# Expert outputs handed back to their tokens: two fp32r products with a 0/1 matrix in place of one float32 product with weights, and the first transposition of h moved behind the next up product

## The chip, the cores and the metric

The kernel runs on one core of a Trainium2 chip. Its time is the time on the device in microseconds (us), the median of several runs; before the change it is 2474.07 us (three runs, 2473.86 to 2476.77).

## The reference

Two models in a row on 256 tokens of width 1024, all in float32: first two layers with a three-branch mixer, of which the first has a dense SwiGLU and the second a mixture of experts, then two layers with attention. The change lies in the mixture of experts of the second layer. Cut to that:

```python
logits = xf @ w_router                         # 256 tokens, 8 experts
top_logit, top_idx = lax.top_k(logits, 2)
top_w = jax.nn.softmax(top_logit, axis=-1)
# for each expert e, on the tokens that chose it:
y = (silu(xs @ w_gate[e]) * (xs @ w_up[e])) @ w_down[e]     # 1024 -> 2816 -> 1024
out[token] += weight * y                        # each token gets its two experts' rows
x = layernorm(alpha * x + out)
```

## The kernel before

The tokens that chose an expert are worked on in items of up to 128 (CAP) rows. A loop on every engine (`Fori(0, n_items)`) turns once for each item. The weights of an item are 33 panels of 1 MB, in the order gate 0, up 0, gate 1, up 1, gate 2, up 2, down 0, gate 3, up 3, down 1 and so on (11 chunks of 256 hidden columns). SyncE loads each panel into one of seven places when TensorE has given back the panel that was there (L689).

**Precision.** A float32 matmul is done as three fp32r matmuls: each operand is split into a high part (a copy written as fp32r) and a low part (the difference). `mm3` (L1068) issues high x high, high x low, low x high. The high part of a panel is written by ScalarE (`widen`, L1758) and the low part by VectorE (`split_panel`, L2457). Only the first panel of an item is widened by VectorE (L2455). So each panel passes ScalarE, VectorE and TensorE in this order, and every engine takes its instructions strictly as they are listed.

**Gather.** `gather` (L1163) multiplies the tokens, x_tm, with one_hot (1 where a token sits in a row of the item) in plain float32; ScalarE and VectorE split the result into xe_hi and xe_lo.

**Chunks.** For chunk s TensorE computes gate and up (`wide`, L1137) into bank s % 2. ScalarE applies silu (L1762), VectorE multiplies (`product`, L2461), TensorE transposes the product (`turn`, L1146), ScalarE writes the high part of h (`hidden_hi`, L1766), VectorE the low part (`hidden_lo`, L2465). `last` (L1153) multiplies with down and sums all chunks in banks 2 and 3. In a step s TensorE's list is: gate s, turn(s - 1), up s, last(s - 2). ScalarE's list is: widen gate s + 1, hidden_hi(s - 1), widen up s + 1, silu(s), widen down s - 1. VectorE's list is: split gate s + 1, hidden_lo(s - 1), split up s + 1, product(s), split down s - 1. Before the chunk loop both also do up 0, and VectorE gate 0.

**Scatter.** The output of an item is copied from banks 2 and 3 into y_sb by ScalarE at the start of the next turn (`y_out`, L1775). There, behind gate 0 and up 0, TensorE multiplies it with `spread` (L1171): for each of the two blocks of 128 tokens and each of the two halves of the columns one plain float32 matmul of 512 columns, into banks 4 to 7. spread is the transposed `weighted`, a one-hot times the routing weight, which VectorE makes at step 2 (L2511), TensorE transposes near the end of the turn (L1207) and ScalarE copies (L1801). VectorE adds the four results to acc (`accumulate`, L2480) behind the split of up 1. The transpositions of h write banks 6 and 7, so before turn(0) TensorE waits until accumulate has read them (acc_read, L1198). In the first turn spread is zero and banks 2 and 3 are filled by two matmuls (L1188). Behind the loop there is one more scatter and sum, then the layer norm.

Of the kernel before, what the change touches and what calls it, by code (L numbers as in the profile page):

```python
# [20 lines left out]
P = 128  # L21
D = 1024
# [329 lines left out]
mix_mm mixed wout_mm ln_x ln_std ln_z ln_x_done  # L352
router_mm router_w router_exp gu_full act_out h_ready y_full y_read up_full relu_out h_ready_2 y_full_2 y_read_2
counts_mm items_ready one_hot routed_mm xe_hi xe_lo spread split_hi split x_split h_made h_hi mem_std mem_inv mem_x mem_turned mem_xT
panel_wide e_first panel_split e_prod e_turned e_hT_hi y_half y_whole y_sb scatter_mm acc_read
rms_ss rms_std rms_x attn_proj attn_read qk_std qk_ready turnq_mm turnq_act
cmp_tb cmp_h_mm cmp_mid cmp_mid_mm cmp_h cmp_o_mm cmp_kv cmp_k_std cmp_k_ready cmp_kT_mm cmp_kT cmp_v cmp_s_mm cmp_s cmp_e cmp_p
score_mm score_max score_exp pT_mm pT pv_mm pv_read proj2_mm x_done nsa_gates
# [3 lines left out]
def program(nc, weights, consts, attn_consts, cols, mids, rows, ln_rows, x, mem, out):  # L362
    ctx = ExitStack()
    with ctx:
        def sb(name, *shape, stack=ctx, dtype=F32):
            return stack.enter_context(nc.sbuf_tensor(name, [P, *shape], dtype))
# [116 lines left out]
        table = sb("table", ITEMS + 2, stack=moe)  # L483
        table_i = moe.enter_context(nc.sbuf_tensor("table_i", [P, ITEMS + 2], I32))
        one_hot = sb("one_hot", TT, CAP, stack=moe)
        weighted = sb("weighted", TT, CAP, stack=moe)
        spread = sb("spread", TT, P, stack=moe)
        xe_hi = sb("xe_hi", KB, CAP, stack=moe, dtype=F32R)
        ring_more, ring_more_lo = twice_named("ring_more", RING, PANEL, stack=moe)
        y_sb = sb("y_sb", D, stack=moe)  # L490
        acc = sb("acc", TT, D, stack=moe)
        moe.close()
        split.close()

# [219 lines left out]
        def _(pe):  # L714
# [412 lines left out]
            def moe_pe():  # L1127


                def weights_of(part, s, item):  # L1130

                    k = moe_order(part, s)
                    pe.wait_ge(S["panel_split"], item * PER_ITEM + (MIXER_SPLITS + k + 1))
                    panels.step()
                    return panel_hi(k), moe_panel(k, item)[1]

                def wide(part, s, item):  # L1137

                    w = weights_of(part, s, item)
                    o = bank[s % 2][:, (0 if part == "gate" else FCH):][:, 0:FCH]  # L1140
                    for kb in range(KB):
                        ins = mm3(o, (xe_hi[:, kb, :], xe_lo[:, kb, :]), [t[:, kb * PC:(kb + 1) * PC] for t in w], start=(kb == 0), stop=(kb == KB - 1))
                    if part == "up":
                        ins.then_inc(S["gu_full"], 1)

                def turn(s, item):  # L1146

                    pe.wait_ge(S["e_prod"], item * FF_CHUNKS + (s + 1))
                    for m in range(2):
                        ins = pe.transpose(bank[6 + s % 2][:, m * CAP:(m + 1) * CAP], h_tm[:, s % 2, m * P:(m + 1) * P], ident)  # L1150
                    ins.then_inc(S["e_turned"], 1)

                def last(s, item):  # L1153
                    w = weights_of("down", s, item)
                    pe.wait_ge(S["h_ready"], item * FF_CHUNKS + (FF_CHUNKS + s + 1))
                    for h in range(2):
                        for m in range(2):
                            ins = mm3(bank[2 + h][:], [t[:, s % 3, m, 0:CAP] for t in (hT_hi, hT_lo)], [t[:, m * D + h * 512:][:, 0:512] for t in w],
                                      start=(s == 0 and m == 0), stop=(s == FF_CHUNKS - 1 and m == 1))
                        if s == FF_CHUNKS - 1:  # L1160
                            ins.then_inc(S["y_whole"] if h else S["y_half"], 1)

                def gather():  # L1163

                    for kb in range(KB):
                        for tt in range(TT):
                            ins = pe.matmul(bank[4 + kb // 4][:, kb % 4 * CAP:][:, 0:CAP], x_tm[:, tt, kb * P:(kb + 1) * P], one_hot[:, tt, :],  # L1167
                                            start=(tt == 0), stop=(tt == TT - 1))
                    return ins

                def scatter(n):  # L1171

                    pe.wait_ge(S["spread"], n + 1)
                    for h in range(2):
                        pe.wait_ge(S["y_sb"], 2 * n + (h + 1))
                        for tt in range(TT):
                            ins = pe.matmul(bank[4 + 2 * h + tt][:], spread[:, tt, :], y_sb[:, h * 512:(h + 1) * 512], start=True, stop=True)  # L1177
                        ins.then_inc(S["scatter_mm"], 1)

                pe.wait_ge(S["items_ready"], 1)  # L1180
                n_items = pe.value_load(table_i[0:1, 0:1], min_val=N_EXPERTS, max_val=ITEMS)
                pe.wait_ge(S["one_hot"], 1)
                pe.wait_ge(S["ln_x_done"], 2 * DEPTH - 1)
                pe.wait_ge(S["attn_read"], MEM_PANELS)
                gather().then_inc(S["routed_mm"], 1)

                pe.wait_ge(S["spread"], 1)
                pe.matmul(bank[2][:], spread[:, 0, :], x_tm[:, 0, 0:512], start=True, stop=True).then_inc(S["y_half"], 1)  # L1188
                pe.matmul(bank[3][:], spread[:, 0, :], x_tm[:, 0, 0:512], start=True, stop=True).then_inc(S["y_whole"], 1)
                with pe.Fori(0, n_items) as item:  # L1190
                    pe.wait_ge(S["xe_lo"], item + 1)
                    wide("gate", 0, item)
                    wide("up", 0, item)
                    scatter(item)
                    for s in range(1, FF_CHUNKS):
                        wide("gate", s, item)
                        if s == 1:
                            pe.wait_ge(S["acc_read"], item + 2)  # L1198
                        turn(s - 1, item)
                        wide("up", s, item)  # L1200
                        if s >= 2:
                            last(s - 2, item)
                    turn(FF_CHUNKS - 1, item)
                    pe.wait_ge(S["one_hot"], item + 2)
                    gather()
                    for tt in range(TT):
                        ins = pe.transpose(bank[1][:, tt * P:(tt + 1) * P], weighted[:, tt, :], ident)  # L1207
                    ins.then_inc(S["routed_mm"], 1)
                    last(FF_CHUNKS - 2, item)
                    last(FF_CHUNKS - 1, item)  # L1210
                pe.wait_ge(S["xe_lo"], n_items + 1)
                scatter(n_items)
                pe.wait_ge(S["acc_read"], n_items + 2)
# [285 lines left out]
        def _(act):  # L1499
# [247 lines left out]
            def moe_act():  # L1747
# [26 lines left out]

                def y_out(n):  # L1775
                    act.wait_ge(S["y_half"], n + 1)
                    act.activation(y_sb[:, 0:512], bank[2][:], ACT.Copy).then_inc(S["y_sb"], 1)
                    act.wait_ge(S["y_whole"], n + 1)
                    act.activation(y_sb[:, 512:], bank[3][:], ACT.Copy).then_inc(S["y_sb"], 1)

                act.activation(spread[:], cst[:, 0:TT * P].rearrange("p (t k) -> p t k", t=TT), ACT.Copy, scale=0.0).then_inc(S["spread"], 1)
                tokens_hi(0)
# [223 lines left out]
        def _(dve):  # L2006
# [431 lines left out]
            def moe_dve():  # L2438
# [29 lines left out]
                def tokens_lo(n):  # L2468
# [3 lines left out]
                                  xe_hi[:, 4 * h:4 * h + 4, :].bitcast(F32), ALU.subtract)  # L2472
                    ins.then_inc(S["xe_lo"], 1)

                def accumulate(n):
                    for h in range(2):
                        dve.wait_ge(S["scatter_mm"], 2 * n + (h + 1))
                        for tt in range(TT):
                            a = acc[:, tt, h * 512:(h + 1) * 512]
                            ins = tt_(a, a, bank[4 + 2 * h + tt][:], ALU.add)  # L2480
                    ins.then_inc(S["acc_read"], 1)
                    dve.wait_ge(S["acc_read"], n + 2)

                for tt in range(TT):
                    ins = ts_(one_hot[:, tt, :], count, item_pos[:, tt, 0:1], None, ALU.is_equal)
                ins.then_inc(S["one_hot"], 1)
# [3 lines left out]
                with dve.Fori(0, n_items) as item:  # L2490
                    split_panel("gate", 0, item)
                    split_panel("up", 0, item)
                    for s in range(FF_CHUNKS):
                        if s + 1 < FF_CHUNKS:
                            split_panel("gate", s + 1, item)
# [10 lines left out]
                        if s == 2:  # L2506

                            dve.wait_ge(S["routed_mm"], item + 1)
                            for tt in range(TT):
                                ts_(one_hot[:, tt, :], count, item_pos[:, tt, bass.ds(item + 1, 1)], None, ALU.is_equal)  # L2510
                                ins = ts_(weighted[:, tt, :], count, item_pos[:, tt, bass.ds(item, 1)], item_w[:, tt, bass.ds(item, 1)],  # L2511
                                          ALU.is_equal, ALU.mult)
                            ins.then_inc(S["one_hot"], 1)
                    hidden_lo(FF_CHUNKS - 1, item)
                    split_panel("down", FF_CHUNKS - 1, item)
                    tokens_lo(item + 1)
                accumulate(n_items)

            def mlp_dve(kind, l, n_chunks, base, per_step, n_split):
# [499 lines left out]
```

## Time and profile before

| | |
|---|---|
| median of three runs | 2474.07 us |
| time of the profiled execution | 2474.79 us |
| its span, first to last instruction | 2473.0 us |
| mean granted TensorE clock | 0.974 of full speed |
| TensorE busy, matmul | 2371.8 us |
| VectorE busy | 1724.9 us |
| ScalarE busy | 958.3 us |

The profile is of one execution. A busy time is the time in which an engine had an instruction at work; matmuls overlap one another, so their durations are longer than their distance. A view in order of time gives start, duration, engine, line and tiles. Brackets behind a row give how long the engine was idle before it and what released it. The span leaves out 1.8 us around the instructions.

### The profile page before, as it was taken

The page shows a single profiled execution, that of the slowest core. Times are in us where ns is not written, and L with a number is a line of the kernel's source. Part 1 is how long each engine was busy: PE and PEld are TensorE (multiplying, and loading weights), DVE is VectorE, ACT ScalarE, POOL GpSimd, SP SyncE. Part 2 cuts the span into 40 slices and gives each one's busy share as a digit, 9 for nine tenths or more (in the row PEclk, how much of TensorE's full clock was granted, in tenths as well). Part 3 has the DMA queues.
Part 4 walks back from the last instruction along what each step waited for, and adds up shares of the span by engine and source line. Part 5 has one row for each costly group of instructions (what it writes and reads, how often), then busy time and mean ns, then how long its engine had stood idle before and what let it go on. Part 6 is the DMA issues. An engine that isn't in the chain of part 4 may idle for free.

```text
span 2473.0 us, 42815 instructions
## 1 busy us (share of the span) xinstructions
PE 2371.8 (96%) x17534; PEld 2102.8 (85%) x17534; DVE 1724.9 (70%) x1887; ACT 958.3 (39%) x1165; POOL 6.4 (0%) x14
## 2 busy tenths in 40 slices
PE   8999989979999989999999999999999999999998
PEld 6899769977998679899998999998876899876997
DVE  4775267776763378879888798887455777565776
ACT  4324010024333246767667676675234100232000
POOL 0000000000000000000000000000000000000000
PEclk9999999988999989999999999999989999999999
DMA  5222335542322559889898898986421455321454
GB/s 201 104 104 103 119 137 187 187 146 94 120 100 90 204 189 345 334 326 338 336 344 335 324 339 334 345 336 244 166 102 52 156 189 187 131 85 68 174 187 151
DMA packets 68603, 495.18 MB, mean 200 GB/s; under 512 B 7584, under 2 KB 7712, under 8 KB 9104
## 3 DMA queue, kind: packets, MB, share of 16 engines
q1 hardware_dynamic: 67072, 485.57, 53.3%
q0 software_dynamic: 1424, 8.05, 0.9%
q8 instruction: 83, 1.36, 0.2%
q14 instruction: 24, 0.20, 0.0%
HBM read 492.54 MB, written 1.05 MB: 200 GB/s over the span
## 4 chain that ended last, share of the span: by engine, by line
PE 68%; DVE 5%; ACT 1%; issue 1%; DVEq 0%; ACTq 0%
PE wide L336 26%; PE wide L1072 15%; PE wide L1071 15%; PE wide L1167 1%; PE wide L1177 1%; PE wide L892 1%; PE wide L1369 1%; PE wide L1355 1%; PE wide L1150 1%; DVE ring_more_lo L2457 1%; PE wide L1318 0%; PE wide L727 0%; PE wide L1352 0%; DVE ring_hi L2455 0%; DVE ring_lo L2536 0%
## 5 line engine op out<-in xcount | busy, mean ns | idle before, releaser
L336 PE MATMUL wide<-ring_hi,xe_hi 128*128 128x256 f32 x1088 | 315.4, 290 | 7.1 <-DVE ring_more_lo L2457 7.1
L1072 PE MATMUL wide<-ring_hi,xe_lo 128*128 128x256 f32 x1088 | 305.5, 281 | 0.0
L336 PE MATMUL wide<-ring_hi,hT_hi 128*128 128x512 f32 x664 | 262.7, 396 | 2.5 <-DVE ring_lo L2536 2.5
L1072 PE MATMUL wide<-ring_hi,hT_lo 128*128 128x512 f32 x664 | 262.2, 395 | 0.0
L336 PE MATMUL wide<-xT_hi,ring_hi 128*128 128x256 f32 x864 | 244.4, 283 | 7.0 <-DVE xT_lo L2040 4.7
L2457 DVE TENSOR_TENSOR ring_more_lo<-ring_more,ring_hi 128x2048 fp32r<-128x2048 f32 x96 | 219.2, 2290 | 41.2 <-ACT ring_hi L1758 40.2
L2457 DVE TENSOR_TENSOR ring_lo<-ring,ring_hi 128x2048 fp32r<-128x2048 f32 x96 | 219.9, 2290 | 35.0 <-ACT ring_hi L1758 33.6
L1072 PE MATMUL wide<-xT_hi,ring_lo 128*128 128x256 f32 x864 | 244.2, 283 | 0.0
L1071 PE MATMUL wide<-xT_lo,ring_hi 128*128 128x256 f32 x864 | 244.0, 282 | 0.0
L336 PE MATMUL wide<-mix_xT_hi,mix_hi 128*128 128x256 f32 x768 | 229.4, 299 | 5.2 <-DVE xT_lo L2040 5.2
L1071 PE MATMUL wide<-xT_lo,mix_hi 128*128 128x256 f32 x768 | 221.3, 288 | 0.0
L1072 PE MATMUL wide<-mix_xT_hi,ring_lo 128*128 128x256 f32 x768 | 220.8, 287 | 0.0
L336 PEld LDWEIGHTS wide<-ring_hi,xe_hi 128*128 128x128 f32 x1088 | 205.5, 189 | 15.0 <-DVE ring_more_lo L2457 11.0
L2536 DVE TENSOR_TENSOR ring_lo<-ring,ring_hi 128x2048 fp32r<-128x2048 f32 x94 | 215.5, 2292 | 3.2
L1071 PE MATMUL wide<-ring_lo,hT_hi 128*128 128x512 f32 x536 | 210.2, 392 | 0.0
L1721 ACT ACTIVATE gate_s<-wide 128x512 f32<-128x512 f32 x43 | 25.8, 600 | 475.5 <-PE wide L1072 475.5
L1072 PEld LDWEIGHTS wide<-ring_hi,xe_lo 128*128 128x128 f32 x1088 | 206.5, 190 | 0.0
L1071 PE MATMUL wide<-ring_more_lo,xe_hi 128*128 128x256 f32 x704 | 198.3, 282 | 0.0
L336 PE MATMUL wide<-ring,xT 128*128 128x256 f32 (+1 forms) x752 | 188.5, 411 | 1.0 <-DVE xT L2022 1.0
L1758 ACT ACTIVATE ring_hi<-ring 128x2048 fp32r<-128x2048 f32 x96 | 183.5, 1912 | 14.8 <-PE wide L336 14.8
L1758 ACT ACTIVATE ring_hi<-ring_more 128x2048 fp32r<-128x2048 f32 x88 | 168.8, 1919 | 49.9 <-PE wide L336 49.0
L2534 DVE CAST ring_hi<-ring 128x2048 fp32r<-128x2048 f32 x94 | 115.3, 1226 | 102.1 <-DMA ring<-in_weights 101.9
(459 smaller groups left out, 5097.0 us busy)
## 6 DMA issues: line engine op xcount, KB each, us to landing
ring<-in_weights SPq DMA_DIRECT2D x316, 1024.0 KB, 4.8
ring_more<-in_weights SPq DMA_DIRECT2D x120, 1024.0 KB, 4.8
xT<-in_weights SPq DMA_DIRECT2D x24, 1024.0 KB, 4.9
ln_row<-in_ln_rows POOLq DMA_DIRECT2D x4, 1024.0 KB, 6.2
x_tm<-in_x SPq DMA_DIRECT2D x1, 1024.0 KB, 5.9
qkT<-in_mem POOLq DMA_DIRECT2D x1, 1024.0 KB, 5.3
out<-x_tm SPq DMA_DIRECT2D x1, 1024.0 KB, 4.0
cst<-in_consts SPq DMA_DIRECT2D x1, 1009.5 KB, 11.9
```

The lines of the kernel that those rows point to most:

```text
L336: ins = self.pe.matmul(out, lhsT, rhs, start=start, stop=stop)
L892: ins = pe.matmul(o, lhs[hs, h, :], chunk_ident[hs] if turned else rhs[hs, h, :], start=True, stop=True)
L1071: pe.matmul(out, lhsT[0], rhs[1], start=False, stop=False)
L1072: return pe.matmul(out, lhsT[1], rhs[0], start=False, stop=stop)
L1150: ins = pe.transpose(bank[6 + s % 2][:, m * CAP:(m + 1) * CAP], h_tm[:, s % 2, m * P:(m + 1) * P], ident)
L1167: ins = pe.matmul(bank[4 + kb // 4][:, kb % 4 * CAP:][:, 0:CAP], x_tm[:, tt, kb * P:(kb + 1) * P], one_hot[:, tt, :], start=(tt == 0), sto ...
L1177: ins = pe.matmul(bank[4 + 2 * h + tt][:], spread[:, tt, :], y_sb[:, h * 512:(h + 1) * 512], start=True, stop=True)
L1721: act.activation(gate_s[:, slot, :, :], b[:].rearrange("p (m t) -> p m t", m=2), func).then_inc(sems["out"], 1)
L1758: act.activation(panel_hi(k), w, ACT.Copy).then_inc(S["panel_wide"], 1)
L2457: tt_(lo, w, panel_hi(k).bitcast(F32), ALU.subtract).then_inc(S["panel_split"], 1)
L2534: copy(ring_hi[:, slot, :], ring[:, slot, :]).then_inc(S["split_hi"], 1)
L2536: tt_(ring_lo[:, slot, :], ring[:, slot, :], ring_hi[:, slot, :].bitcast(F32), ALU.subtract).then_inc(S["split"], 1)
```

## The change

The matrix that spreads an item's rows to the tokens no longer holds the weights. It is an exact 0/1 matrix (in_slot, transposed into spread), of type fp32r. The item's output is split into y_hi (ScalarE, as y_sb before) and y_lo (VectorE, the new `outputs_lo`), and each of the four products becomes two fp32r matmuls, with y_hi and with y_lo. The routing weight is applied by VectorE: accumulate becomes acc = bank * item_by + acc, with item_by, the column of this item's weights, copied at step 2 of the turn and cleared before the first. outputs_lo stands behind the split of up 0 in the loop, and ahead of the last accumulate behind it. TensorE's turn(0), with the wait for accumulate, moves from between gate 1 and up 1 to behind up 1. The two matmuls that fill banks 2 and 3 ahead of the first turn become four of 256 columns.

```diff
-        weighted = sb("weighted", TT, CAP, stack=moe)
-        spread = sb("spread", TT, P, stack=moe)
+        in_slot = sb("in_slot", TT, CAP, stack=moe)
+        spread = sb("spread", TT, P, stack=moe, dtype=F32R)
+        item_by = sb("item_by", TT, 1, stack=moe)
-        y_sb = sb("y_sb", D, stack=moe)
+        y_hi = sb("y_hi", D, stack=moe, dtype=F32R)
+        y_lo = sb("y_lo", D, stack=moe, dtype=F32R)
@@ TensorE, scatter
-                        pe.wait_ge(S["y_sb"], 2 * n + (h + 1))
+                        pe.wait_ge(S["y_lo"], 2 * n + (h + 1))
                         for tt in range(TT):
-                            ins = pe.matmul(bank[4 + 2 * h + tt][:], spread[:, tt, :], y_sb[:, h * 512:(h + 1) * 512], start=True, stop=True)
+                            pe.matmul(bank[4 + 2 * h + tt][:], spread[:, tt, :], y_hi[:, h * 512:(h + 1) * 512], start=True, stop=False)
+                            ins = pe.matmul(bank[4 + 2 * h + tt][:], spread[:, tt, :], y_lo[:, h * 512:(h + 1) * 512], start=False, stop=True)
@@ TensorE, before the loop
-                pe.matmul(bank[2][:], spread[:, 0, :], x_tm[:, 0, 0:512], start=True, stop=True).then_inc(S["y_half"], 1)
-                pe.matmul(bank[3][:], spread[:, 0, :], x_tm[:, 0, 0:512], start=True, stop=True).then_inc(S["y_whole"], 1)
+                nothing = spread[:].rearrange("p t k -> p (t k)")
+                for b, sem in ((2, "y_half"), (3, "y_whole")):
+                    for h in range(2):
+                        ins = pe.matmul(bank[b][:, h * T:(h + 1) * T], spread[:, 0, :], nothing, start=True, stop=True)
+                    ins.then_inc(S[sem], 1)
@@ TensorE, the chunks
                     for s in range(1, FF_CHUNKS):
                         wide("gate", s, item)
+                        if s > 1:
+                            turn(s - 1, item)
+                        wide("up", s, item)
                         if s == 1:
                             pe.wait_ge(S["acc_read"], item + 2)
-                        turn(s - 1, item)
-                        wide("up", s, item)
+                            turn(0, item)
                         if s >= 2:
                             last(s - 2, item)
@@ VectorE
+                def outputs_lo(n):
+                    for h in range(2):
+                        dve.wait_ge(S["y_sb"], 2 * n + (h + 1))
+                        a = slice(h * 512, (h + 1) * 512)
+                        tt_(y_lo[:, a], bank[2 + h][:], y_hi[:, a].bitcast(F32), ALU.subtract).then_inc(S["y_lo"], 1)
@@ accumulate
-                            ins = tt_(a, a, bank[4 + 2 * h + tt][:], ALU.add)
+                            ins = stt(a, bank[4 + 2 * h + tt][:], item_by[:, tt, :], a, ALU.mult, ALU.add)
@@ the loop
+                dve.memset(item_by[:], 0.0)
                 with dve.Fori(0, n_items) as item:
                     split_panel("gate", 0, item)
                     split_panel("up", 0, item)
+                    outputs_lo(item)
@@ step 2
+                            copy(item_by[:], item_w[:, :, bass.ds(item, 1)])
-                                ins = ts_(weighted[:, tt, :], count, item_pos[:, tt, bass.ds(item, 1)], item_w[:, tt, bass.ds(item, 1)],
-                                          ALU.is_equal, ALU.mult)
+                                ins = ts_(in_slot[:, tt, :], count, item_pos[:, tt, bass.ds(item, 1)], None, ALU.is_equal)
@@ behind the loop
+                outputs_lo(n_items)
                 accumulate(n_items)
```

## Rows read from the trace of the kernel before

**Rows 1.** The page, part 1: busy microseconds, share of span, instructions, by engine.
```profile
PE 2371.8 (96%) x17534; PEld 2102.8 (85%) x17534; DVE 1724.9 (70%) x1887; ACT 958.3 (39%) x1165; POOL 6.4 (0%) x14
```

**Rows 2.** ScalarE in order of time: start, duration, instruction; two turns of the loop.
```profile
1000.89 0.58 ACT L1777 ACTIVATE y_sb<-wide 128x512 f32<-128x512 f32 x1
...
1104.03 0.58 ACT L1777 ACTIVATE y_sb<-wide 128x512 f32<-128x512 f32 x1
```

**Rows 3.** Instructions on tile spread: count, duration min/median/max in ns, first and last start.
```profile
L1177 PE MATMUL wide<-y_sb,spread x72: 590/592/595, 904.6 to 1726.6; 128*128 128x512 f32 x72
L1801 ACT ACTIVATE spread<-wide x8: 391/391/391, 997.0 to 1719.2; 128x256 f32<-128x256 f32 x8
```

**Rows 4.** TensorE's waits in one turn; the same turn's window, DMA share last but one.
```profile
PE wide L336 <- DVE ring_more_lo L2457: 0.4, 1, 0.4
...
1002.00:1104.00 102.00, 102.00 (x722) 94.33 (x723) 86.90 (x66) 70.08 (x60) 0.00 (x0) 1.00 0.89 335
```

**Rows 5.** TensorE in order of time, behind the scatter of the second turn.
```profile
1007.70 3.60 PE L1177 MATMUL wide<-y_sb,spread 128*128 128x512 f32 x8
...
1013.95 0.38 PE L1150 MATMUL wide<-cst,gate_s 128*128 128x128 f32 x2
...
1017.01 0.28 PE L336 MATMUL wide<-ring_hi,xe_hi 128*128 128x256 f32 x1
...
1019.86 0.38 PE L1150 MATMUL wide<-cst,gate_s 128*128 128x128 f32 x2
...
1022.90 0.40 PE L336 MATMUL wide<-ring_hi,hT_hi 128*128 128x512 f32 x1
...
1023.60 0.40 PE L336 MATMUL wide<-ring_hi,hT_hi 128*128 128x512 f32 x1
```

**Rows 6.** ScalarE in order of time, same stretch; idle time before an instruction in brackets.
```profile
1014.36 0.39 ACT L1766 ACTIVATE hT_hi<-wide 128x256 fp32r<-128x256 f32 x1 [4.28 <-PE wide L1150]
1014.64 1.91 ACT L1758 ACTIVATE ring_hi<-ring 128x2048 fp32r<-128x2048 f32 x1
1017.21 0.39 ACT L1762 ACTIVATE gate_s<-wide 128x256 f32<-128x256 f32 x1 [0.66 <-PE wide L1072]
```

**Rows 7.** VectorE in order of time, same stretch.
```profile
1008.32 0.42 DVE L2461 TENSOR_TENSOR gate_s<-gate_s,wide 128x256 f32<-128x256 f32 x1 [1.68 <-ACT gate_s L1762]
...
1010.85 2.47 DVE L2480 TENSOR_TENSOR acc<-acc,wide 128x512 f32<-128x512 f32 x4
1013.45 2.29 DVE L2457 TENSOR_TENSOR ring_lo<-ring,ring_hi 128x2048 fp32r<-128x2048 f32 x1
...
1016.59 2.29 DVE L2457 TENSOR_TENSOR ring_lo<-ring,ring_hi 128x2048 fp32r<-128x2048 f32 x1 [0.51 <-ACT ring_hi L1758]
1018.80 0.42 DVE L2461 TENSOR_TENSOR gate_s<-gate_s,wide 128x256 f32<-128x256 f32 x1
1019.44 2.29 DVE L2457 TENSOR_TENSOR xT_lo<-xT,ring_hi 128x2048 fp32r<-128x2048 f32 x1 [0.22 <-ACT ring_hi L1758]
```

**Rows 8.** Two instructions of VectorE by line: count, duration min/median/max in ns.
```profile
L2471 DVE TENSOR_TENSOR xe_lo<-wide,xe_hi x18: 680/686/692, 891.5 to 1719.9; 128x512 fp32r<-128x512 f32 x18
...
L2583 DVE SCALAR_TENSOR_TENSOR x_tm<-wide,rs,x_tm x8: 740/742/751, 2111.4 to 2467.8; 128x512 f32<-128x512 f32 x8
```

**Rows 9.** ScalarE, VectorE and TensorE in order of time behind the loop.
```profile
1723.75 0.60 ACT L1779 ACTIVATE y_sb<-wide 128x512 f32<-128x512 f32 x1 [0.78 <-PE wide L1072]
...
1727.18 1.29 DVE L2480 TENSOR_TENSOR acc<-acc,wide 128x512 f32<-128x512 f32 x2 [0.43 <-PE wide L1177]
...
1728.52 0.33 PE L1493 MATMUL wide<-cst 128*128 128x128 f32 x1 [1.38 <-DVE acc L2480]
```

**Rows 10.** A TensorE wait of another stage; windows behind pauses, granted clock third from last.
```profile
PE wide L336 <- DVE ring_lo L2536: 2.2, 1, 2.2
...
352.40:355.60 3.20, 3.20 (x17) 3.20 (x17) 3.17 (x3) 0.00 (x0) 0.00 (x0) 0.50 0.90 315
...
1728.60:1732.00 3.40, 3.40 (x17) 3.01 (x18) 2.90 (x8) 0.30 (x1) 0.00 (x0) 1.00 0.60 193
```

More of the change, by code:

```diff
@@ L354 @@
 counts_mm items_ready one_hot routed_mm xe_hi xe_lo spread split_hi split x_split h_made h_hi mem_std mem_inv mem_x mem_turned mem_xT
-panel_wide e_first panel_split e_prod e_turned e_hT_hi y_half y_whole y_sb scatter_mm acc_read
+panel_wide e_first panel_split e_prod e_turned e_hT_hi y_half y_whole y_sb y_lo scatter_mm acc_read
 rms_ss rms_std rms_x attn_proj attn_read qk_std qk_ready turnq_mm turnq_act
@@ L1206, in moe_pe @@
                     for tt in range(TT):
-                        ins = pe.transpose(bank[1][:, tt * P:(tt + 1) * P], weighted[:, tt, :], ident)
+                        ins = pe.transpose(bank[1][:, tt * P:(tt + 1) * P], in_slot[:, tt, :], ident)
                     ins.then_inc(S["routed_mm"], 1)
@@ L1776, in y_out @@
                     act.wait_ge(S["y_half"], n + 1)
-                    act.activation(y_sb[:, 0:512], bank[2][:], ACT.Copy).then_inc(S["y_sb"], 1)
+                    act.activation(y_hi[:, 0:512], bank[2][:], ACT.Copy).then_inc(S["y_sb"], 1)
                     act.wait_ge(S["y_whole"], n + 1)
-                    act.activation(y_sb[:, 512:], bank[3][:], ACT.Copy).then_inc(S["y_sb"], 1)
+                    act.activation(y_hi[:, 512:], bank[3][:], ACT.Copy).then_inc(S["y_sb"], 1)
                 act.activation(spread[:], cst[:, 0:TT * P].rearrange("p (t k) -> p t k", t=TT), ACT.Copy, scale=0.0).then_inc(S["spread"], 1)
```

## The prediction

> **What bounds the kernel now.** I read the page's busy shares first: TensorE is busy for 96% of the span, so a shorter TensorE instruction can only pay where TensorE is the last to be ready [rows 1]. The change lies in the expert loop. The loop's period is the distance between two starts of the same ScalarE instruction one item apart, 1104.03 - 1000.89 = 103.14 us [rows 2], and the copy into spread at the end of each turn occurs 8 times [rows 3]: 8 turns and a ninth scatter behind them. In one turn the view of waits shows TensorE waiting 0.4 us, once, and the window of the same turn a DMA share of 0.89 [rows 4]. So TensorE bounds the loop; the others have slack, VectorE with 86.9 us of 102 the least. Last I read the three engines in order of time over the stretch behind the scatter, since what counts is by how much VectorE and ScalarE are ahead at each handover. Times there are written without the leading 1000.
>
> **What is removed.** The scatter is 8 matmul records in 3.60 us, one of them 592 ns long [rows 3, 5]: the pitch is (3.60 - 0.59)/7 = 0.43, eight of them 3.44 us. The new scatter has 8 fp32r matmuls of 512 columns. The down projection is made of just such ones: three from 22.90 to 23.60, 0.70/3 = 0.232 each [rows 5]; eight make 1.86 us. TensorE's own work falls by 1.58 us an item. If that were all, nine times 1.58 = 14.2 us would go.
>
> **What VectorE gets.** outputs_lo is two instructions of 128x512 from PSUM; the nearest row is xe_lo, 686 ns [rows 8], or 1.29 us for a pair that overlaps by 0.08. They stand behind the split of up 0, and VectorE sits idle there later for 1.68 us before product(0) [rows 7]; 1.29 fits, and y_lo is ready near 5.4, ahead of the scatter at 7.70. The scaled sum takes 742 ns in the same form (PSUM, a column of scalars, SBUF) [rows 8]; four end to end are at most 2.97 us against the present 2.47 [rows 7], with the overlap of before 2.7: +0.25 to +0.5. The copy of item_by and the plainer one-hot are some 0.1 us net in a stretch where VectorE has over 1 us in hand. The ring of slots frees two panels 1.58 earlier and one somewhat later, and no row of TensorE waits for a panel's landing: nothing there. The clearing of item_by and the shorter first products stand once ahead of the loop; bounds 0 and 0.2, I take 0.1.
>
> **What the moved turn costs.** Before, turn(0) stands between gate 1 and up 1, at 13.95; now behind up 1. Its time on TensorE is the same, but on it hangs a chain, which I follow in the rows of before: turn(0) at 13.95; ScalarE's hT_hi at 14.36 (+0.41), which is queued ahead of the widening of up 2, at 14.64 (+0.28), 1.91 long to 16.55; VectorE's split of up 2 at 16.59, 2.29 long; product(1) behind it at 18.80, ending at 19.22 [rows 5 to 7]. TensorE's turn(1) needs product(1). From turn(0) to the end of product(1) this is 19.22 - 13.95 = 5.27 us. Before, TensorE had up 1 and gate 2 to do meanwhile and came to turn(1) at 19.86: 0.64 us after the product, so the chain was hidden.
>
> After: the scatter begins at 7.70 as before; up 1 begins at 13.95 - 1.58 = 12.37; gate 2, of the same 24 products, takes 19.86 - 17.01 = 2.85 [rows 5], so turn(0) is at 15.22 (and 17.01 - 13.95 - 2.85 = 0.21 long). hT_hi 15.63, widening 15.91 to 17.82, split 17.86, product(1) 20.07 to 20.49 (silu(1), behind the widening, is through at 18.2: not the last). The handover back to TensorE is 0.05 behind the last sum of the loop, where nothing had to be loaded [rows 9]; here the weights are the product itself, and I take 0.15. So turn(1) starts at 20.64. TensorE alone would be there at 19.86 - 1.58 = 18.28. It stands still for 2.36 us, and the item is not 1.58 shorter but 20.64 - 19.86 = 0.78 us **longer**. Part of the stall is taken a step earlier: the sum begins at 10.85, ends near 13.6 with the dearer form, and the split of gate 2, which starts at 13.45 now [rows 7], ends at about 16.0, against TensorE's 15.43. That is 0.6 of the same 2.36, not more of it.
>
> What is queued behind these waits: on ScalarE behind hT_hi the widening of up 2, silu(1), down 0, gate 3; on VectorE behind the split of up 2 product(1) and the split of down 0. Carried on at the pitch of 2.2 us a panel (16.59, product in between, 19.44), VectorE has down 0 at 22.7 against TensorE's need at 23.7, gate 3 at 24.9 against 26.4, up 3 at 27.4 against 29.4. Nothing else is late, and after the one-hots VectorE is ahead by more than 1.5 us again. The rest of the turn is TensorE's, moved by +0.78. Bounds of this term: 1.58 less if the chain hid again, and 1 us more if the sum or the split of gate 2 came out on the path too. I take +0.78, 8 times: +6.2.
>
> **The last scatter.** It has nothing to overlap with. Before, the second half of y starts being copied at 1723.75, scatter and sum end at 1728.47, where the norm's statistics and TensorE's 1728.52 follow [rows 9]. After: y_lo's second half from 1724.36 to 1725.04, its four products to 1726.0 and 0.15 to drain, then two sums of 0.74 to 1727.6: -0.8 us.
>
> **Sum.** +6.2 - 0.8 + 0.1 = +5.5 us. The profiled execution took 2474.79 us for its span of 2473.0; it would take 2480.3. The median of the runs shown is 0.7 lower, 2474.07, which gives 2479.6.
>
> **Rivals.** *Faster: the stall does not come.* If hT_hi did not hold up product(1), the whole 1.58 would come through: 8 x 1.58 + 0.8 = 13.4 us, 2460.6. It decides from 1.58 us of slack in the chain; the rows show 0.64 before the turn is moved, and the chain starts 15.22 - 13.95 = 1.27 us later while TensorE comes 1.58 earlier. Only an order other than the listing's would allow it. A weaker form, in which a microsecond of the chain overlaps, gives between -2 and +3.
>
> *Slower by more: the clock falls in the stall.* The pause before turn(1) is 20.64 - 18.9 = 1.7 us long, that before gate 2 0.6. In the dense products of another stage a pause of 2.20 us was followed by a stretch at a granted clock of 0.50, that is 1.2 GHz; after the pause of 1.38 us behind the last scatter the clock stayed at 1.00, 2.4 GHz [rows 9, 10]. 1.7 lies between. A stretch of at least 3.2 us at half speed [rows 10] loses 1.6 us or a little more; in half of the items that is +6.4 to +7, hence 2486; in all, 2493. The Trainium skill, TensorE: Matmul & The Clock Gate, section A second HAM failure mode: psum-queue depth-cycling, says that micro-idles between groups of matmuls, when frequent, make the clock swing between its two levels. By that rule the 16 new pauses would speak for this case; the loop's present pause of 0.4 us an item leaves the clock at 1.00 [rows 4], so the trace agrees only that short ones do no harm.
>
> *Another wait takes over: y_lo holds up the scatter.* It is ready 2.3 us ahead; it would have to cost four times its row. I give it, with the backlog spoiling a later panel (+1 us an item, 2487), a twentieth.
>
> **How the numbers follow.** No change and a change can be told apart here from about 0.2%, 4.9 us: 2469.1 to 2479.0. The main case has 0.57 and spans +3.5 to +7, so that it lies astride this bound: 0.36 of it slower, 0.21 the same. The clock has 0.14 and the other wait 0.05, both slower. The weaker overlap has 0.12, mostly the same, the full gain 0.12. Slower 0.55, same 0.32, faster 0.13. The range takes in main case, most of the weak overlap and the clock in half of the items: 2473 to 2487.
>
> **What would show it.** Scatter records near 1.9 us an item; TensorE's waits for gate_s, ahead of the transposes, near 1.7 us, 8 times, and for a ring_lo split 0.4 to 0.6, 8 times; hT_hi of chunk 0 as much later; a loop period of 103.9; granted clock 1.00 in the loop. I am wrong if the period is under 103.1, or if TensorE shows no pause at the second turn; a clock below 1.00 in the loop would be the second rival.

## The result: 0.2% slower, as forecast

In 17 runs each the median went from 2476.38 us to 2481.39 us; the ratio is 1.002, 95% interval [1.0013, 1.0028]: 5.0 us, between 3.2 and 6.9. That is over the 0.2% named in the prediction by a hair, and clear of zero. The profiled execution took 2480.85 us for a span of 2479.0 us.

The profile of the changed kernel, first the page's span and busy shares. TensorE is busy 9.1 us less than in [rows 1], although the span is 6.0 us longer: work went and waiting came.

```profile
span 2479.0 us, 42850 instructions
PE 2362.7 (95%) x17534; PEld 2105.5 (85%) x17534; DVE 1736.7 (70%) x1914; ACT 957.9 (39%) x1165; POOL 6.4 (0%) x14
```

TensorE's waits over the whole expert loop (engine, line, tile, what it waited for: us in total, times, longest). The first and third are new. The first is turn(1), which waits for product(1); the third is gate 2, which waits for its split. The second is the wait at the start of a turn that [rows 4] show: seven of 0.4 and the first, of 5.6 (4.3 before, which costs nothing: from the write of zeros into spread to the first copy of y it is 11.85 us, 11.84 before).

```profile
PE wide L1152 <- DVE gate_s L2469: 11.4, 8, 1.4
PE wide L336 <- DVE ring_more_lo L2465: 8.4, 8, 5.6
PE wide L336 <- DVE ring_lo L2465: 3.3, 8, 0.4
```

ScalarE in order of time (start, duration, instruction). The first and last row are the copies that [rows 2] gave for before; the two between answer to [rows 6].

```profile
1003.46 0.58 ACT L1785 ACTIVATE y_hi<-wide 128x512 fp32r<-128x512 f32 x1
...
1018.29 0.38 ACT L1774 ACTIVATE hT_hi<-wide 128x256 fp32r<-128x256 f32 x1 [5.58 <-PE wide L1152]
1018.57 1.91 ACT L1766 ACTIVATE ring_hi<-ring 128x2048 fp32r<-128x2048 f32 x1
...
1107.67 0.58 ACT L1785 ACTIVATE y_hi<-wide 128x512 fp32r<-128x512 f32 x1
```

The period of this turn, from one copy of y to the next, is 104.21 us, 1.07 more than before. ScalarE is idle for 5.58 us ahead of hT_hi (4.28 before), because the transposition that it waits for comes later, and the widening of up 2 stands behind it.

TensorE over the same stretch, with [rows 5] for before. Eight scatter products from 1010.31 to 1012.18 take 1.87 us instead of 3.44. Then turn(0) and turn(1); the figures in brackets are TensorE's waits ahead of gate 2 and of turn(1).

```profile
1010.31 0.40 PE L1179 MATMUL wide<-y_hi,spread 128*128 128x512 f32 x1
...
1012.18 0.28 PE L336 MATMUL wide<-ring_hi,xe_hi 128*128 128x256 f32 x1
...
1017.87 0.38 PE L1152 MATMUL wide<-cst,gate_s 128*128 128x128 f32 x2
1018.66 0.38 PE L336 MATMUL wide<-ring_hi,xe_hi 128*128 128x256 f32 x1 [0.41 <-DVE ring_lo L2465]
...
1023.19 0.44 PE L1152 MATMUL wide<-cst,gate_s 128*128 128x128 f32 x2 [1.42 <-DVE gate_s L2469]
```

And VectorE, with [rows 7] for before: y_lo, the scaled sum, the splits of gate 2 and of up 2, product(1). The split of up 2 now waits 1.38 us for its widening, where it waited 0.51.

```profile
1006.61 1.28 DVE L2487 TENSOR_TENSOR y_lo<-wide,y_hi 128x512 fp32r<-128x512 f32 x2
...
1013.47 2.72 DVE L2494 SCALAR_TENSOR_TENSOR acc<-wide,item_by,acc 128x512 f32<-128x512 f32 x4
1016.31 2.29 DVE L2465 TENSOR_TENSOR ring_lo<-ring,ring_hi 128x2048 fp32r<-128x2048 f32 x1
...
1020.51 2.29 DVE L2465 TENSOR_TENSOR ring_lo<-ring,ring_hi 128x2048 fp32r<-128x2048 f32 x1 [1.38 <-ACT ring_hi L1766]
1022.72 0.41 DVE L2469 TENSOR_TENSOR gate_s<-gate_s,wide 128x256 f32<-128x256 f32 x1
```

Behind the loop (ScalarE's copy, then VectorE; [rows 9] for before) there was a gain. The copy of the second half of y starts at 1733.56, y_lo's second half runs 1734.19 to 1734.88, and the norm's statistics start at 1737.61: 4.05 us behind the copy instead of 4.75.

```profile
1733.56 0.60 ACT L1787 ACTIVATE y_hi<-wide 128x512 fp32r<-128x512 f32 x1 [0.79 <-PE wide L1074]
...
1734.19 0.69 DVE L2487 TENSOR_TENSOR y_lo<-wide,y_hi 128x512 fp32r<-128x512 f32 x1 [0.70 <-ACT y_hi L1787]
1734.80 2.77 DVE L2494 SCALAR_TENSOR_TENSOR acc<-wide,item_by,acc 128x512 f32<-128x512 f32 x4
1737.61 2.47 DVE L2336 BATCH_NORM_STATS2 stat<-acc 128x6 f32<-128x512 f32 x4
```

For the comparisons below I measure two more things in each trace. The **stage** is the time from ScalarE's write of zeros into spread to the first norm statistics behind the loop; it holds all that the change touches but the clearing of item_by (0.06 us). The **pitch** is the mean distance of two products of 256 columns that follow each other in the second turn, 20 us behind the copy of y and later (some 360 to 380 distances). The **period** and the positions of turn(0) and turn(1) are those of the second turn, counted from the start of the copy of y.

| kernel | median us | ratio to before, 95% | turn(0) | turn(1) | pitch ns | period | stage |
|---|---|---|---|---|---|---|---|
| before | 2476.38 | | 13.06 | 18.97 | 117.8 | 103.14 | 845.7 |
| changed | 2481.39 | 1.002 [1.0013, 1.0028] | 14.41 | 19.73 | 118.6 | 104.21 | 853.2 |
| turn(0) in its old place | 2474.89 | 0.9992 [0.9983, 1.0001] | 12.92 | 18.86 | 118.6 | 103.23 | 845.3 |
| the move alone | 2499.05 | 1.0081 [1.0068, 1.0095] | 15.92 | 21.23 | 117.8 | 105.48 | 867.1 |
| up 2 widened first | 2471.2 | 0.9978 [0.9969, 0.9987] | 14.46 | 18.30 | 118.6 | 102.74 | 841.5 |
| sum in halves | 2467.0 | 0.9959 [0.9946, 0.9973] | 11.58 | 17.50 | 118.6 | 101.93 | 835.5 |
| item_by padded | 2483.09 | 1.0025 [1.0015, 1.0035] | 14.38 | 19.69 | 118.2 | 103.99 | 851.6 |
| before plus 8 bytes | 2482.89 | 1.0021 [1.0012, 1.003] | 13.10 | 19.00 | 118.6 | 103.39 | 847.6 |
| halves and padded | 2471.87 | 0.9966 [0.9952, 0.9981] | 11.54 | 17.48 | 118.2 | 101.79 | 834.1 |
| item_by in stat | 2479.83 | 1.0015 [1.0006, 1.0024] | 14.32 | 19.63 | 117.8 | 103.88 | 850.8 |
| halves, item_by in stat | 2459.88 | 0.9935 [0.9921, 0.9949] | 11.53 | 17.49 | 117.8 | 101.77 | 833.6 |

Each ratio is to the kernel before on the same chip, so it is the number to compare, not the median.

### The profile page after: what moved, and what is told of

It reads as the page before. It is cut to its first block, busy times and chain, and to the rows that moved or that the text cites. A ratio compares the mean times of both kernels' runs of the same rounds, so it can differ in the third digit from the quotient of the medians.

```text
span 2479.0 us, 42850 instructions
## 1 busy us (share of the span) xinstructions
PE 2362.7 (95%) x17534; PEld 2105.5 (85%) x17534; DVE 1736.7 (70%) x1914; ACT 957.9 (39%) x1165; POOL 6.4 (0%) x14
## 4 chain that ended last, share of the span: by engine, by line
PE 67%; DVE 5%; issue 2%; ACT 2%; DVEq 0%; ACTq 0%
PE wide L336 26%; PE wide L1074 15%; PE wide L1073 15%; PE wide L1169 1%; PE wide L894 1%; PE wide L1377 1%; PE wide L1152 1%; PE wide L1363 1%; DVE ring_more_lo L2465 1%; ACT ring_hi L1766 1%; PE wide L1360 1%; PE wide L1326 0%; PE wide L729 0%; DVE ring_hi L2463 0%; PE wide L1337 0%
```

## The experiments

**1. Is it the move? The change without it.**

```diff
                         wide("gate", s, item)
-                        if s > 1:
-                            turn(s - 1, item)
-                        wide("up", s, item)
                         if s == 1:
                             pe.wait_ge(S["acc_read"], item + 2)
-                            turn(0, item)
+                        turn(s - 1, item)
+                        wide("up", s, item)
```

> The change without its move: fp32r scatter, weight in the sum, but turn(0) between gate 1 and up 1 as before. Theory (the moved turn starts a chain over hT_hi, the widening and split of up 2 and product(1), and turn(1) waits for its end): turn(0) now waits for the sum, which ended 12.73 us behind the copy of y in the changed kernel, so it stands at about 12.8 instead of 14.4 (13.06 before); TensorE then reaches turn(1) at about 18.8 without a wait (18.97 before, 19.73 changed). Loop period 103.2 (102.9 if the 0.3 us that the changed kernel loses behind turn(1) goes too), against 104.21; time 2 to 10 us under the changed kernel and within 3 us of the kernel before. Rival (the fp32r scatter or outputs_lo, not the move, cost the item its 1.07 us): the period stays near 104.2.

turn(0) came at 12.92 and turn(1) at 18.86, with no wait between them. The waits of TensorE show one new line only, turn(0) waiting for the sum:

```profile
PE wide L1152 <- DVE acc L2492: 9.1, 8, 1.1
PE wide L336 <- DVE ring_more_lo L2463: 8.4, 8, 5.5
```

The stage is 8.0 us shorter than the changed kernel's. So the loss is the move's. But without the move the gain of 1.58 us is not there either: turn(0) comes only 0.14 us earlier than before, so the wait for the sum takes 1.4 of it (the view shows 1.1, since it counts from the end of the last matmul). The ratio, 0.9992, is not told apart from 1. The two edits answer to each other, and neither place of turn(0) lets the scatter's gain through as the sum stands.

**2. The move alone, on the kernel before.**

```diff
                         wide("gate", s, item)
-                        if s == 1:
-                            pe.wait_ge(S["acc_read"], item + 2)
-                        turn(s - 1, item)
+                        if s > 1:
+                            turn(s - 1, item)
                         wide("up", s, item)
+                        if s == 1:
+                            pe.wait_ge(S["acc_read"], item + 2)
+                            turn(0, item)
```

> The kernel before with only the move of turn(0) and its wait behind up 1. Theory: turn(0) at 13.06 + 2.85 = 15.9 us behind the copy of y, the chain of 5.27 us and the handover set turn(1) to 21.3 instead of 18.97: +2.3 us an item, period 105.4, time +18 us (2494). TensorE shows a wait of about 2.3 us ahead of turn(1). Rival (the move costs nothing, the loss is of the split scatter): period 103.1, time as before. Of the drift of 0.3 us behind turn(1): if it comes from the later VectorE work it is here too, if it comes from the new tile item_by (8 bytes, which shift the tiles behind it) it is not.

turn(0) at 15.92, turn(1) at 21.23, period 105.48: as reckoned within 0.1 us a turn. TensorE's wait for product(1):

```profile
PE wide L1150 <- DVE gate_s L2463: 16.8, 8, 2.1
```

The stage is 21.5 us longer, 2.8 more than 8 x 2.34 = 18.7. The rest is the second rival of the prediction, which shows itself here: behind the first and the fifth of these eight pauses of 2.1 us the granted clock was at half, 1.2 GHz, for at least the 3.2 to 3.3 us of the windows below. The first and the fifth turn lost 3.8 and 3.7 us against before, the other six 2.3, so the two stretches cost 1.5 and 1.4. TensorE at the end of the first pause, and windows behind the first, from within the second, and behind the fifth (granted clock third from last):

```profile
922.49 0.69 PE L1150 MATMUL wide<-cst,gate_s 128*128 128x128 f32 x2 [2.10 <-DVE gate_s L2463]
```
```profile
922.50:925.80 3.30, 3.30 (x16) 3.30 (x17) 3.30 (x2) 3.21 (x3) 0.00 (x0) 0.50 0.35 89
1028.00:1031.20 3.20, 1.74 (x15) 1.74 (x16) 3.20 (x3) 3.20 (x4) 0.00 (x0) 1.00 0.41 151
1345.80:1349.00 3.20, 3.13 (x15) 3.13 (x16) 3.20 (x3) 3.20 (x3) 0.00 (x0) 0.50 0.28 51
```

Over 800 us this is lost in the rounding of the window's clock; it takes windows as short as the stretch to see it. In the changed kernel, with pauses of 1.4, no stretch between 904 and 1724 is at half speed. The pitch stayed at 117.8 here, so VectorE's work coming later does not cause the slower products.

**3. Which link of the chain? ScalarE widens up 2 ahead of hT_hi.**

```diff
-                        if s:
+                        if s > 1:
                             hidden_hi(s - 1, item)
                         if s + 1 < FF_CHUNKS:
                             widen("up", s + 1, item)
+                        if s == 1:
+                            hidden_hi(0, item)
                         silu(s, item)
```

> The changed kernel; on ScalarE the widening of up 2 goes ahead of hT_hi of chunk 0. Theory: the chain from turn(0) loses the widening: 0.41 + 0.39 for hT_hi, then VectorE's hT_lo 0.33, the split of up 2 2.21, product(1) 0.42, handover 0.06, that is 3.85 us instead of 5.3; turn(1) at 18.3 us behind the copy of y (19.73 in the changed kernel, 18.97 before). Period 102.8 with the drift of 0.3, time some 11 us under the changed kernel, 4 to 6 us under the kernel before. Rival (the wait ahead of turn(1) is set by silu(1) or by VectorE's sum alone): period 104.2 still.

turn(1) at 18.30, period 102.74, stage 11.8 us under the changed kernel's. TensorE's wait for product(1) is gone from the view, and only gate 2's wait for its split is left beside the one at the start of a turn:

```profile
PE wide L336 <- DVE ring_lo L2467: 3.3, 8, 0.4
PE wide L336 <- DVE ring_more_lo L2467: 2.8, 7, 0.4
```

A swap of two instructions on an engine that is busy 39% of the time turns the change from a loss into a gain (0.9978). The wait was for the order of ScalarE's list, not for ScalarE's time.

Behind the loop this kernel shows that a shorter pause can be followed by half speed too. TensorE's pause behind the last scatter, and a window behind it (granted clock 0.50):

```profile
1726.28 0.34 PE L1501 MATMUL wide<-cst 128*128 128x128 f32 x1 [1.50 <-DVE acc L2496]
```
```profile
1726.60:1729.80 3.20, 3.20 (x9) 2.54 (x8) 2.70 (x8) 0.30 (x1) 0.00 (x0) 0.50 0.50 189
```

Five kernels have this pause at 1.50 us. Here and in "item_by padded" the clock fell behind it, in the changed kernel, in "turn(0) in its old place" and in "item_by in stat" it stayed at 1.00, as it did behind the pauses of 1.62 to 1.65 us in the three kernels with the sum in halves.

**4. Let all of the scatter's gain through.** The transposes write banks 6 and 7. With the halves of the scatter swapped, those two banks are summed first, turn(0) needs only that, and VectorE does the second half of the sum behind product(1). The edit against the changed kernel, cut to the lines that carry it:

```diff
-    bank[4 + 2 * h + tt]                                   # scatter and sum
+    bank[6 - 2 * h + tt]
-                    pe.wait_ge(S["acc_read"], item + 2)
+                    pe.wait_ge(S["acc_read"], 2 * item + 2)     # turn(0) again between gate 1 and up 1
-                            accumulate(item)
+                            accumulate(item, 0)                 # acc_read counts halves
...
                             product(s, item)
+                            if s == 1:
+                                accumulate(item, 1)
                             split_panel("down", s - 1, item)
```

> The changed kernel with turn(0) in its old place, the halves of the scatter in swapped banks (first half into 6 and 7, which the transposes write, second into 4 and 5), turn(0) waiting only for the first half's sum, and the second half's sum behind product(1). Theory: the first half's sum ends near 11.5 us behind the copy of y, ahead of gate 1's end (11.6), so turn(0) waits for nothing; the split of gate 2 is through by 13.8, ahead of TensorE's 14.6; turn(1) at 17.4 (18.97 before). All of the scatter's 1.58 us comes through: period 101.6 to 101.9, time 2462 to 2466, 9 to 13 us under the kernel before. Rival (VectorE's added work or the later panels bound the item, so that the wait comes back elsewhere): period 102.5 or more.

Period 101.93, a hair over the range; 2467.0 us, 1.0 over it, though the gain of 9.3 us over the kernel before on the same chip lies inside. Ratio 0.9959. The wait ahead of turn(1) is gone, and turn(1) stands at 17.50. VectorE of that kernel: half a sum, the split of gate 2 at 14.72 - 3.39 = 11.33 behind the copy of y instead of 12.85, and the other half behind product(1).

```profile
1013.40 1.40 DVE L2492 SCALAR_TENSOR_TENSOR acc<-wide,item_by,acc 128x512 f32<-128x512 f32 x2
1014.72 2.28 DVE L2463 TENSOR_TENSOR ring_lo<-ring,ring_hi 128x2048 fp32r<-128x2048 f32 x1
...
1019.83 0.41 DVE L2467 TENSOR_TENSOR gate_s<-gate_s,wide 128x256 f32<-128x256 f32 x1
1020.16 1.40 DVE L2492 SCALAR_TENSOR_TENSOR acc<-wide,item_by,acc 128x512 f32<-128x512 f32 x2
```

**5. The rest: 0.3 us a turn behind turn(1).** At turn(1) the changed kernel is 0.76 us behind, as forecast; at the end of the second turn 1.07. The difference grows evenly, by 0.12 us in the step behind turn(1) and then by 0.01 to 0.07 a step, with no wait. The products themselves are slower: of gate 3 the first and the twenty-second start 2.46 us apart before and 2.49 us in the changed kernel (TensorE, first before, then changed):

```profile
1025.68 0.28 PE L336 MATMUL wide<-xT_hi,xe_hi 128*128 128x256 f32 x1
...
1028.14 0.28 PE L336 MATMUL wide<-xT_hi,xe_hi 128*128 128x256 f32 x1
```

```profile
1029.09 0.28 PE L336 MATMUL wide<-xT_hi,xe_hi 128*128 128x256 f32 x1
...
1031.58 0.28 PE L336 MATMUL wide<-xT_hi,xe_hi 128*128 128x256 f32 x1
```

Every kernel with item_by as a tile of its own has the slower pitch, and the move alone has not. I tested the place in memory, in five kernels; the first edit below was made to the changed kernel and to "sum in halves", the second to the kernel before, the third to the changed kernel and to "sum in halves".

```diff
         item_by = sb("item_by", TT, 1, stack=moe)
+        sb("item_pad", 14, stack=moe)            # item_by padded; also: halves and padded
```
```diff
         spread = sb("spread", TT, P, stack=moe)
+        sb("two_more", 2, stack=moe)             # before plus 8 bytes
```
```diff
-        item_by = sb("item_by", TT, 1, stack=moe)
+        item_by = stat[:, 50:50 + TT].rearrange("p (t o) -> p t o", o=1)   # item_by in stat
```

> The changed kernel with an unused tile of 14 floats behind item_by, so that the tiles behind it (xe_hi, ring_more, acc) lie 64 bytes further than before the change instead of 8. Theory (the 8 bytes put the operands of the expert products off their old alignment, and each 256-column product takes 118.6 instead of 117.8 ns, some 0.3 us an item): pitch 117.8 ns, period 103.9, time 2 to 3 us under the changed kernel's. The wait ahead of turn(1) stays. Rival (the pitch follows from VectorE's later or added work, or from the fp32r type of spread): pitch 118.6, period 104.2.

> The kernel before with nothing but an unused tile of 2 floats behind spread, which moves xe_hi, ring_more, y_sb and acc by 8 bytes. Theory: pitch of the 256-column products 118.6 ns instead of 117.8, period 103.4 instead of 103.14, time some 2 us more. Rival (placement plays no part): pitch 117.8, period 103.14.

> The kernel with the sum in halves and turn(0) in its old place, and item_by padded to 64 bytes. Theory: both gains add: period 101.93 - 0.3 = 101.6, time 2463 to 2465, 11 to 13 us under the kernel before. Rival (placement plays no part): period 101.9, as without the padding.

> The changed kernel with item_by in two free columns of the tile stat, so that xe_hi, ring_more and acc lie at exactly the addresses of the kernel before. Theory (the slower products come from the placement alone): pitch of the 256-column products 117.8 ns, as before; period 104.21 - 0.27 = 103.9, so that only the 0.76 us of the chain are left over the 103.14 of before. Stage from the copy of zeros into spread to the norm's statistics 851.3 us (853.2 changed, 845.7 before). Rival (the fp32r type of spread or the added VectorE work has a part in it): pitch over 118.0.

> The kernel with the sum in halves and turn(0) in its old place, with item_by in stat. Theory: pitch 117.8, period 101.93 - 0.27 = 101.66, stage 833.3 us (835.5 with item_by as a tile of its own, 845.7 before): a 12.4 us shorter stage. The time of the whole kernel, 2464, can differ by some 3 us either way, as the half-speed stretches of the stages behind the loop (37 us of them in the trace before, 55 in two others) fall otherwise.

The kernel before with 8 unused bytes and nothing else has the pitch 118.6 and the period 103.39: 0.25 us of the 0.31. With item_by in stat, so that xe_hi, ring_more and acc lie where they lay, the changed kernel is back at 117.8 and 103.88 (gate 3, this kernel: 2.45 us).

```profile
1031.02 0.28 PE L336 MATMUL wide<-xT_hi,xe_hi 128*128 128x256 f32 x1
...
1033.47 0.28 PE L336 MATMUL wide<-xT_hi,xe_hi 128*128 128x256 f32 x1
```

So the placement is shown. My form of it, that the 64-byte alignment decides, fell: with 64 bytes instead of 8 the pitch is 118.2 in both kernels, and a part of the loss stays. Over the eight turns the padding gives back 1.7 of the 2.6 us that item_by in stat gives back, and 1.4 of 1.9 in the kernels with the sum in halves. Nor is it one slowdown of all products. From each product of ring_hi with xe_lo to the next one it is 117.1 ns before, 118.2 changed and 117.1 with 64 bytes, but from each one with xe_hi 117.9, 118.8 and 119.1 (means of the loop's turns behind the first). Which of the shifted tiles matters, and by which rule, stays open.

Three of the five expectations missed clearly in the time of the whole kernel, and the last by 1 us. The padded one, expected 2 to 3 us better than the changed kernel, came out at 1.0025; before plus 8 bytes lost 5.9 us instead of 2; halves and padded, expected at 2463 to 2465, took 2471.87. Their stages moved as the pitch lets expect (-1.6, +1.9 and -1.4 us against their twins). The difference lies outside the stage, in code that is the same in all kernels. The padded kernel took 2.2 us more ahead of the stage and 1.8 more behind it than the changed kernel. Behind the loop it is 744.5 us before, 741.4 in the changed kernel and 750.1 in before plus 8 bytes. In that last kernel a stretch of the attention ran at half speed: its products start 1.3 us later than those of before ahead of the stretch, and 6.3 us later behind it. In order, that kernel's window, and a window of the kernel before that holds the same work:

```profile
1889.00:1902.00 13.00, 12.50 (x56) 11.57 (x55) 5.54 (x13) 2.52 (x6) 0.00 (x0) 0.50 0.00 0
```
```profile
1885.00:1900.00 15.00, 12.31 (x75) 8.99 (x75) 7.11 (x17) 5.08 (x16) 0.00 (x0) 1.00 0.16 52
```

"Halves and padded" has the same stretch and again 750.1 us behind the loop; this is why its ratio, 0.9966, is worse than that of its unpadded twin, 0.9959, though its stage is 1.4 us shorter. Its nine runs fall into two groups: six, the profiled one among them, took 2470.4 to 2474.5 us, and three 2462.6 to 2463.3, as expected or just below. So the same kernel can come out either way, and its median says little on the placement.

The last kernel, with the sum in halves and item_by in stat, beats both: 2459.88 us, ratio 0.9935 [0.9921, 0.9949], 16 us under the kernel before, and 1 us beyond the stated margin. Its stage is 12.1 us shorter; the other 4 us are behind the loop (740.7 against 744.5 us), in code that none of the edits touches; whether the earlier end of the loop brings them is not shown. In its loop the one wait of before is left:

```profile
PE wide L336 <- DVE ring_more_lo L2463: 2.8, 7, 0.4
```

## Why the prediction was right, and where it was off

- *TensorE bounds the loop, so the chain behind the scatter decides.* Right: the wait views of the first three experiments show nothing else.
- *The scatter from 3.44 to 1.86 us.* Right: 1.87.
- *outputs_lo fits in VectorE's idle time; the dearer sum costs 0.25 to 0.5.* Right: 1.28 us in place, idle time ahead of product(0) down from 1.68 to 0.84; the sum 2.72 instead of 2.47.
- *The moved turn starts a chain of 5.27 us.* From turn(0) at 1017.87 to the end of product(1) at 1023.13 it was 5.26. turn(0) came 0.08 later than worked out (14.41 against 14.33) and the handover took 0.06 instead of my 0.15, so the two cancel; turn(1) stood at +0.76 against +0.78. Without a stall turn(1) would have stood at 18.97 - 1.57 = 17.40, so TensorE lost 2.33 us against my 2.36. The move alone lost the same (experiment 2). The view of waits shows 0.41 and 1.42 of it, where I had expected 0.6 and 1.7, since it counts from the end of the last matmul.
- *Nothing else is late behind it, so the item is +0.78.* Here the sum was off: +1.07 in the second turn, 1.0 to 1.1 in the others, 8.25 us for the eight against the +6.2 forecast. No wait came, as said, but the products were 0.7% slower. This is the mis-sized term, by 2.0 us, and it had no place among the rivals: I took the rest of the turn as TensorE's unchanged work, and did not ask where the tiles would lie.
- *The last scatter -0.8 us.* From the start of the copy of the second half (1733.56) to the statistics 4.05 us, against 1728.50 - 1723.75 = 4.75 before: -0.7. The +0.1 that I allowed ahead of the loop measured 0.01.
- *Sum.* Stage: +5.5 forecast, 8.25 - 0.70 = +7.6 in the traces. Kernel: +5.5 forecast, +5.0 [3.2, 6.9] measured. That these agree so well is partly luck: in the profiled execution the stages around the loop, which the change does not touch, gave 1.5 us back (1.5 more ahead of it, 3.1 less behind).
- *The clock falls in the stall.* Not in the changed kernel: behind its pauses of 1.42 us, eight of them, the clock stayed at 1.00. The mechanism is real, though: with 2.1 us it came in two of eight turns (experiment 2), as behind the 2.20 us of [rows 10]. Nor is a shorter pause always harmless: the one behind the last scatter grew with the change from 1.38 to 1.50 us, and at that length half speed followed in two of five kernels (experiment 3). The Trainium skill (TensorE: Matmul & The Clock Gate, A second HAM failure mode: psum-queue depth-cycling) says that micro-idles between groups of matmuls, when frequent, make the clock swing between its levels. The trace of experiment 2 agrees in two of its eight turns; the changed kernel's 16 new pauses in the loop, of 0.41 and 1.42 us, left the clock at 1.00.
- *Faster by 13 us.* It needed another order, as said. That order exists: with it the stage is 10.2 us shorter (experiment 4), and with the old places in memory as well 12.1 us (experiment 5).

## What to carry over

When an instruction is moved later on the engine that bounds, follow what hangs on it through the other engines' lists up to the place where the same engine needs the end of it; the slack is the work of that engine between those two places less the length of the chain. Here it was 0.64 us, and the move took the whole of up 1, 2.85 us, from it. What was saved ahead of both places did not enter: turn(1) lost 2.3 us with the shorter scatter and without it. A gain in a buffer's user comes through only if the buffer's release is split as finely as its next user needs it. Put small new tiles where they shift nothing, and compare a stage, not the whole kernel, when the effect is a few tenths of a per cent.

## What was unexpected of the hardware

- Eight bytes more in front of the operands of the expert products made TensorE's 256-column products 118.6 ns apart instead of 117.8 (before plus 8 bytes); 64 bytes more, 118.2.
- Behind a pause of 2.1 us between dense products the clock fell to half in two of eight cases, behind one of 1.50 us in two of five, behind 1.62 to 1.65 us in none of three, and behind 1.34 to 1.43 us in none of 27. So the length of the pause alone does not decide it; what else does is not shown.
- Half-speed stretches in the attention behind the loop are not bound to a place in the code. The same code behind the loop took from 740.6 to 750.1 us in eleven traces, with 26 to 53 us of it at half speed; that it goes by when the loop ends would fit, but I did not test it. Nine of the ten runs of before plus 8 bytes took 2480.6 to 2486.3 us (the tenth 2476.6), against 2473.3 to 2481.3 of the kernel before on the same chip, while "halves and padded" fell into two groups.
